# A float32 model kernel: where the attention values, the attention projection and the convolution's norm stand in the mixing layers

## What is computed

```python
u = h @ w_in[i]                                     # q, k, v, convolution input, two gates
y_attn = sliding_window_attention(q, k, v, sinks[i], rel_bias) @ w_attn_proj[i]
h1 = val * jax.nn.sigmoid(gate)                     # 512 channels
h1 = depthwise_conv(h1, dw) + db                    # 31 taps along the tokens
y_conv = jax.nn.silu(layer_norm(h1, g, b)) @ w_conv_proj[i]
mix = (jax.nn.sigmoid(ga) * y_attn + jax.nn.sigmoid(gc) * y_conv) @ w_out[i]
h = layer_norm(ALPHA * h + mix, ln1_g[i], ln1_b[i])
```

## Time and profile before

| | |
|---|---|
| median of 3 runs | 1739.08 us (1737.29 to 1739.76) |
| span of the profiled execution | 1735.9 us |
| its mean granted TensorE clock | 0.983 of full speed |
| TensorE busy | 1678.5 us, 97% of the span |
| VectorE busy | 1189.9 us, 69% |
| ScalarE busy | 949.9 us, 55% |
| GpSimd busy | 616.9 us, 36% |
| mean DMA rate | 196 GB/s; 326 to 346 GB/s from about 1345 us to about 1690 us |

### The profile page before, as it was taken

How to read it: one execution, slowest core, us unless ns; L and a number is a source line. 1 busy time by engine, 2 the same in 40 slices (tenths; PEclk the granted TensorE clock), 3 DMA queues, 4 the chain that set the end, 5 groups by cost and what they waited for, 6 DMA issues and landing times.

```text
span 1735.9 us, 29864 instructions
## 1 busy us (share of the span) xinstructions
PE 1678.5 (97%) x12148; PEld 1561.4 (90%) x12148; DVE 1189.9 (69%) x1766; ACT 949.9 (55%) x1298; POOL 616.9 (36%) x438
## 2 busy tenths in 40 slices
PE   8999999999989999999999999999899999999997
PEld 7988999998889999987999999988898888888885
DVE  5665655556555545897775555798777888788895
ACT  4556564335655634555454433545447777777774
POOL 4133442012324401133020001121047787886863
PEclk8999999999999999999999999999989999999999
DMA  8432445554334555532335544533327989888992
GB/s 297 190 120 98 160 173 183 190 177 166 120 122 170 195 184 183 177 128 98 130 122 198 180 173 170 171 139 121 111 109 281 338 332 338 326 332 330 346 344 111
DMA packets 50206, 339.90 MB, mean 196 GB/s; under 512 B 5575, under 2 KB 7839, under 8 KB 10351
## 3 DMA queue, kind: packets, MB, share of 16 engines
q1 hardware_dynamic: 47344, 328.79, 52.1%
q0 software_dynamic: 2720, 9.13, 1.7%
HBM read 336.76 MB, written 1.13 MB: 195 GB/s over the span
## 4 chain that ended last, share of the span: by engine, by line
PE 78%; DVE 10%; ACT 7%; issue 3%; POOL 2%; DMA 0%; DVEq 0%; SPq 0%; ACTq 0%; POOLq 0%
PE bank L481 13%; PE bank L483 13%; PE bank L482 13%; PE bank L906 4%; PE bank L907 4%; PE bank L908 4%; DVE CA L1896 3%; DVE wl L1570 3%; ACT wh L1125 3%; PE bank L617 3%; PE bank L618 2%; PE bank L619 2%; PE bank L937 2%; PE bank L939 2%; PE bank L938 2%
## 5 line engine op out<-in xcount | busy, mean ns | idle before, releaser
L1570 DVE TENSOR_TENSOR wl<-stg,wh 128x2048 fp32r<-128x2048 f32 (+1 forms) x310 | 680.9, 2202 | 260.9 <-ACT wh L1125 260.1
L1125 ACT ACTIVATE wh<-stg 128x2048 fp32r<-128x2048 f32 x310 | 592.1, 1911 | 210.0 <-PE bank L483 100.5
L481 PE MATMUL bank<-xh,wh 128*128 128x256 f32 (+1 forms) x1322 | 381.4, 288 | 3.2 <-DVE xl L1616 1.7
L483 PE MATMUL bank<-xh,wl 128*128 128x256 f32 (+1 forms) x1322 | 378.3, 286 | 0.0
L482 PE MATMUL bank<-xl,wh 128*128 128x256 f32 (+1 forms) x1322 | 377.3, 285 | 0.0
L2230 POOL TENSOR_TENSOR wl<-stg,wh 128x512 fp32r<-128x512 f32 x132 | 322.8, 2458 | 114.4 <-ACT wh L1125 96.1
L481 PEld LDWEIGHTS bank<-xh,wh 128*128 128x128 f32 x1322 | 250.7, 190 | 7.3 <-issue 6.6
L483 PEld LDWEIGHTS bank<-xh,wl 128*128 128x128 f32 x1322 | 250.8, 190 | 0.0
L482 PEld LDWEIGHTS bank<-xl,wh 128*128 128x128 f32 x1322 | 250.3, 189 | 0.1
L906 PE MATMUL bank<-wh,GH 128*128 128x512 f32 (+3 forms) x400 | 148.2, 370 | 1.5 <-ACT wh L1125 0.8
L908 PE MATMUL bank<-wl,GH 128*128 128x512 f32 (+3 forms) x400 | 146.5, 366 | 0.0
(11 more groups left out here) (319 smaller groups left out, 3438.4 us busy)
## 6 DMA issues: line engine op xcount, KB each, us to landing
stg<-in_w SPq DMA_DIRECT2D x310, 1024.0 KB, 4.8
BT<-bias_scratch POOLq DMA_DIRECT2D x3, 1024.0 KB, 11.0
BT<-bias_scratch POOLq DMA_DIRECT2D x1, 2048.0 KB, 13.0
BB<-bias_scratch POOLq DMA_DIRECT2D x2, 1024.0 KB, 7.4
res<-in_x SPq DMA_DIRECT2D x1, 1024.0 KB, 5.6
stg<-in_w SPq DMA_DIRECT2D x2, 512.0 KB, 7.1
BB<-bias_scratch POOLq DMA_DIRECT2D x2, 512.0 KB, 7.8
out<-res SPq DMA_DIRECT2D x4, 256.0 KB, 3.4
```

What stands on the lines that cost most here:

```text
L481: pe.matmul(out, wh, xh(kt), start=kt == 0, stop=False)
L483: ins = pe.matmul(out, wl, xh(kt), start=False, stop=kt == KT - 1)
L1125: act.activation(WH[u % NW][:, :], stg[u % NS][:, :], ACT.Copy).then_inc(*m.inc("w_high", u))
L1570: vec.tensor_tensor(WL[u % NW][:, 0:n], stg[u % NS][:, 0:n], WH[u % NW][:, 0:n].bitcast(F32), ALU.subtract).then_inc(*m.inc("w_low_v", u))
```

## The change

Three things are altered in the mixing layers.

1. The value products come two steps later than their turns (`BEHIND = DEEP + 2`), in the even steps and ahead of that step's scores and turns. So the pump of a tile first multiplies the values of jobs that were turned in the pump before. The first pump comes one output tile earlier (`FIRST_STEP = 13`).
2. `ap` starts right behind the gates. The four matmuls of the channel mean stand behind `ap`'s first tile and one matmul for the variance behind its fourth.
3. The convolution norm's variance is no longer summed token by token. ScalarE squares with the factor 1/512 in it, GpSimd adds the four tiles of squares (three additions), one matmul with ones sums them over all partitions and spreads the sum at once, and 1/deviation is worked out on whole 128 x 272 tiles: Ln and Exp on ScalarE, then one Newton step in three VectorE instructions. `token_sums`, `deviation`, the diagonals, their matmuls and the copy are gone for this norm, and a `memset` of two small columns too.

```diff
 AHEAD = 3
 DEEP = 5
+BEHIND = DEEP + 2
+FIRST_STEP = 13
...
                 def step(i):
+                    if i % 2 == 0 and 0 < i - BEHIND < len(jobs):
+                        values(i - BEHIND)
                     if i % 2 == 0 and i < len(jobs):
...
-                    v = i - DEEP - 1
-                    if v % 2 and v > 0:
-                        two = jobs[v - 1:v + 1]
...
                 name = f"c{l}"
-                for kt in range(4):
-                    if kt == 0:
+
+                def conv_sums(nt):
+                    if nt == 0:
                         b, old = bank((name, "mean"), ("mean", name))
                         vacant(old)
...
-                token_sums(name, 4, TILES2, "centred_sq", name)
+                        for kt in range(4):
+                            w.wait_ge(*m.of("conv_v", (l, kt, 30)))
+                            ins = pe.matmul(PS[b][:, 0:T], ones, a["CA"][:, kt, 0:T], start=kt == 0, stop=kt == 3)
+                        ins.then_inc(*m.inc("group", (name, "mean")))
+                    if nt == 3:
+                        b, old = bank((name, "var"), ("var_out", name))
+                        vacant(old)
+                        w.wait_ge(*m.of("conv_sq_added", (l, 3)))
+                        pe.matmul(PS[b][:, 0:T], ones, SQ[:, 0, :], start=True, stop=True).then_inc(*m.inc("group", (name, "var")))
+
                 gemm(4, KD, lambda kt: a["MH"][:, kt, lo:T], lambda kt: a["ML"][:, kt, lo:T], n, f"ap{l}", lambda nt: [("attn_gated", (l, nt))],
-                     halves_ready(f"a{l}"), lambda nt: along_columns(name) if nt == 1 else None)
+                     halves_ready(f"a{l}"), conv_sums)
...  ScalarE
-                mean(name, 4)
...
+                sp.enter(sp.at // UT)
+                w.wait_ge(*m.of("group", (name, "mean")))
+                act.activation(BC[:, :], bank((name, "mean"))[:, 0:T], ACT.Copy, scale=1.0 / (4 * P)).then_inc(*m.inc("mean", name))
+                for kt in range(4):
+                    w.wait_ge(*m.of("centred", (name, kt)))
+                    act.activation(SQ[:, kt, :], XC[:, kt, :], ACT.Square, scale=(4 * P) ** -0.5).then_inc(*m.inc("centred_sq", (name, kt)))
+                act.preload_act_table_set(LOG_EXP)
...
-                    if nt != 1:
+                    if nt != 3:
                         return
-                    spread(name, 4)
+                    w.wait_ge(*m.of("var_out", name))
+                    act.activation(SQ[:, 5, :], SQ[:, 4, :], ACT.Ln).then_inc(*m.step("table"))
+                    w.wait_ge(*m.last("table"))
+                    act.activation(BC[:, :], SQ[:, 5, :], ACT.Exp, scale=-0.5).then_inc(*m.inc("guess", name))
...  VectorE
+                def conv_var():
+                    w.wait_ge(*m.of("group", (name, "var")))
+                    vec.tensor_scalar(v, bank((name, "var"))[:, 0:T], LN_EPS, None, ALU.add).then_inc(*m.inc("var_out", name))
...
-                    if nt == 1:
-                        spread(name)
-                        scale_y(name, "clg", l, 4, low)
+                    if nt == 0:
+                        conv_centre()
+                    if nt == 2:
+                        conv_var()
+                    if nt == 3:
+                        conv_root()
+                        conv_scale()
...  GpSimd
+                for kt in range(1, 4):
+                    w.wait_ge(*m.of("centred_sq", (f"c{l}", kt)))
+                    if kt > 1:
+                        w.wait_ge(*m.of("conv_sq_added", (l, kt - 1)))
+                    pool.tensor_tensor(SQ[:, 0, :], SQ[:, 0, :], SQ[:, kt, :], ALU.add).then_inc(*m.inc("conv_sq_added", (l, kt)))
```

More of the change, by code:

```diff
@@ L739, in mix_layer, with values @@
                 tag, done, scored, opened = f"b{l}", [0], [], {}
+                def values(v):
+                    two = jobs[v - 1:v + 1]
+                    nq, c0, hp, n = two[0]["nq"], two[0]["c0"], two[0]["hp"], len(two[0]["chunks"])
+                    w.wait_ge(*m.of("turned_p", (tag, v, "all")))
+                    if v == 1:
+                        w.wait_ge(*m.of("v_turned", (l, 1)))
+                    if hp not in opened:
+                        opened[hp], old = bank(("pair", tag, hp), ("x_low", (f"a{l}", hp)))
+                        held.add(opened[hp])
+                        vacant(old)
+                    for c in range(n):
+                        for k in range(2):
+                            _, wide, val = two[k]["chunks"][c]
+                            ins = pe.matmul(PS[opened[hp]][64 * k:64 * k + 64, c0:c0 + nq], val,
+                                            a["PT"][(v - 1 + k) % 3][0:wide, c, 0:nq], start=c == 0, stop=c == n - 1)
+                    ins.then_inc(*m.inc("group", ("pair", tag, v)))
+                    if two[0]["tt"] == 1:
+                        let_go(opened[hp])
                 def step(i):
+                    if i % 2 == 0 and 0 < i - BEHIND < len(jobs):
+                        values(i - BEHIND)
                     if i % 2 == 0 and i < len(jobs):
@@ L1925, in mix_layer, with conv_centre, conv_root, conv_scale @@
                 walk_late(30, KD, evac)
-                centre(name, CA, 4)
-                for i in range(done[0], len(jobs) + DEEP + 1):
-                    front(i)
-                    back(i)
-                deviation(name, 4)
+                v, t = SQ[:, 4, :], SQ[:, 6, :]
+                def conv_centre():
+                    w.wait_ge(*m.of("mean", name))
+                    for kt in range(4):
+                        vec.tensor_tensor(XC[:, kt, :], CA[:, kt, 0:T], BC[:, :], ALU.subtract).then_inc(*m.inc("centred", (name, kt)))
+                def conv_var():
+                    w.wait_ge(*m.of("group", (name, "var")))
+                    vec.tensor_scalar(v, bank((name, "var"))[:, 0:T], LN_EPS, None, ALU.add).then_inc(*m.inc("var_out", name))
+                def conv_root():
+                    w.wait_ge(*m.of("guess", name))
+                    vec.tensor_tensor(t, BC[:, :], BC[:, :], ALU.mult).then_inc(*m.step("v_step"))
+                    w.wait_ge(*m.last("v_step"))
+                    vec.scalar_tensor_tensor(t, t, -0.5, v, ALU.mult, ALU.mult).then_inc(*m.step("v_step"))
+                    w.wait_ge(*m.last("v_step"))
+                    vec.scalar_tensor_tensor(BC[:, :], t, 1.5, BC[:, :], ALU.add, ALU.mult).then_inc(*m.inc("rstd", name))
+                    w.wait_ge(*m.last("rstd"))
+                def conv_scale():
+                    for kt in range(5):
+                        if kt < 4:
+                            vec.scalar_tensor_tensor(SQ[:, kt, :], XC[:, kt, :], small("clg", l * 4 + kt), BC[:, :], ALU.mult,
+                                                     ALU.mult).then_inc(*m.inc("normed_y", (name, kt)))
+                        if kt > 0:
+                            low(kt - 1)
                 def low(kt):
@@ L2198, in vector_program @@
             ffn_block(1)
-            vec.memset(st6[:, 0:2, 0:8], 1.0).then_inc(*m.step("v_step"))
-            w.wait_ge(*m.last("v_step"))
             split_norm("mean_e", "embg", "embb", 0)
```

88 lines of the change are left out of this document (13 added, 75 removed).

## The result

The changed kernel takes 1719.87 us (median of 4 runs, 1719.25 to 1722.57); the kernel before took 1738.18 us on the same chip (1736.23 to 1739.76). The ratio is 0.9897 with a 95% interval of 0.9884 to 0.991: 18.3 us faster, where 9.9 us were forecast.

What follows compares the result with a forecast made beforehand. TensorE was taken as the bound, except from the gates' end to `o`, where VectorE and ScalarE hand work to each other; 7.0 + 0.8 + 3.6 - 1.5 = 9.9 us off 1739.1 gave 1729.2 us, range 1724 to 1736.

Steps and rivals of the forecast that it cites:

- Part 1 gives 3.6 + 3.4 = 7.0 us: Gates of both mixing layers: value products read copies made a tile earlier, so 7.6 us of waits go; gain 7.0 us.
- VectorE's slack: Gates: VectorE can bear turns 0.8 to 1.0 us later; without slack in the second layer 3.4 us are lost.
- Part 2: From the end of the gates to `o`: an earlier first Silu gains 0.8 us in the first layer, 3.6 in the second.
- T0: The end of the gates, the zero from which the prediction timed `ap`, the norm and the first Silu.
- S: Time of the first Silu, expected 14.1 us (first layer) and 14.0 us (second) after the end of the gates.
- What is late next: Start of `o`: TensorE's wait of 1.9 us for the last low halves grows to 4 to 6 us in each layer.
- Half clock: Start of `o`: TensorE's clock may fall, 1.6 us a layer; 1.5 us taken, one layer of two, bounds 0 and 3.2.
- VectorE gives the first part back: Rival: the gates' gain is lost in the second layer and the clock falls in both; 1734.3 us, chance 0.14.
- only the waiting place moves: Rival: VectorE reaches the centring no earlier in either layer, 1.2 us left; 1737.9 us, no change, chance 0.12.
- turns wait for VectorE: Rival, slower: turns wait for banks `front` reads later, up to 0.9 us in each of 23 pumps; 1748 us, chance 0.07.
- the additions are not held up: Rival: GpSimd's additions slip in ahead of the split, first Silu 2 us earlier in each layer; 1725.2 us, chance 0.10.

Runs made afterwards that it cites:

- Part 1 alone: Kernel before with the changed kernel's later value products and earlier first pump, old norm and old place of `ap`: 1727.10 us, ratio 0.9934.
- part 2 alone: Changed kernel with the value products and first pump back in their old places: 1734.37 us, ratio 0.9992 to the kernel before.
- the filled wait: Kernel before with four spare matmuls ahead of the second value product of each mixing layer: 1736.60 us, ratio 0.9995.
- the second execution: The changed kernel once more, unaltered, on the same chip as the two runs beside it: 1720.93 us, ratio 0.9904 to the kernel before.
- the clock kept up at `o`: Changed kernel with spare matmuls before the waits of `o`'s first tile for its third to last operands: 1720.89 us, ratio 0.9907 to the kernel before.

## Why the prediction was wrong, step by step

**The step that failed is "Part 1 gives 3.6 + 3.4 = 7.0 us".** Its mechanism was right: the waits for `PTb` went, nothing was late in their place, and VectorE could bear it. Its size was taken from "7.6 us in 16 waits", the matmul records, while the weight loads waited 12.0 us (4.4 us of the miss). And the clock behind these waits was left out of the sum: two spells of 1.5 us (3.0 us). The prediction asked whether new waits would bring half clock and never whether the removed ones had, though its row of the gates gave the clock as 0.98, which over 69.88 us is about one such spell. Part 1 alone gave 14.4 us in the gates; part 2 alone showed the gates with the waits and without a spell, and the filled wait without either spell.

**VectorE's slack** held. Its waits for turns fell from 7.7 us to 4.2 in the first layer, those for `MH` from 5.0 and 4.6 to 1.6 and 1.3, as argued.

**Part 2** held to 0.3 us a layer: 13.83 and 14.10 us measured from the gates' end, 14.0 and 14.3 from T0, against 14.1 and 14.0. The additions took 4.46 and 4.77 us (forecast 4.6), though in the first layer the second of them was held up (2.62 us) and not the first (0.80). The page "GPSIMD Engine Reference" of the Trainium skill, section 8, has the contention with VectorE's instructions of two inputs; the trace agrees, and shows besides that VectorE pays too: that split took 2.87 instead of 2.28 us, though in the second layer it took 2.29. The table load of Silu, 823.86 to 825.14, is hidden beside the Newton step, and the Silu, 0.7 us behind it, is released by VectorE's scaling. The drain of the Trainium skill's page "ScalarE: Activation LUTs", section "What ACT_TABLE_LOAD costs", which would have made S 0.7 us later, is not seen in S: 14.04 us behind T0 against 14.1 without it.

**What is late next.** The waits for the mix came: 2.8 and 3.5 us by the matmul records, where 4 to 6 us a layer were named, but 4.5 and 5.0 us by the weight loads in 840 to 850 us and, behind the dots, in 1224 to 1234 us ("issue" is time for which the profile names no releaser):

```profile
PEld bank L483 <- ACT MH L1396: 3.4, 5, 0.8
PEld bank L483 <- issue: 1.1, 2, 0.7
...
PEld bank L483 <- ACT MH L1396: 3.6, 5, 1.1
PEld bank L483 <- issue: 1.4, 2, 0.7
```

Their size was right, and read from the same records that would have mended part 1. Half clock fell on both layers, 1.3 and 2.1 us (1.8 and 0.8 in the second execution), instead of one: 3.3 or 2.6 us where 1.5 were taken, about the upper bound of 3.2. It is the one term that was too small as a loss, and it hid 1 to 2 us of the first error.

**The rivals.** That VectorE gives the first part back and that only the waiting place moves are refuted by the gates and the Silu together; that turns wait for VectorE by the list of waits, which has no such row. That the additions are not held up is refuted too, but it had a point: GpSimd began 0.08 us ahead of the split and one addition slipped in, in the first layer only. Taking them off GpSimd gave about the 2 us a layer that this rival named. None of the rivals gave a time as low as the measured one, and none named the waits' true size.

**What stays open.** The two parts alone give 10.3 and 3.1 us by the medians, 13.4 together, and 12.4 and 2.7 us by the changed stretches, 15.1 together. In the changed kernel the changed stretches give 15.4 and 16.2 us in two executions, the medians 18.3 and 17.3. The half clock ahead of the first mixing layer and the wait for the input differ from one execution to the next, 700.1 to 705.3 us over all kernels here, and the kernel before ran between 1733.2 and 1745.4 us; the median of the changed kernel lies 2.0 us above its first profiled span and 0.5 us below the second, where that of the kernel before lay 3.2 above its own. Whether the change has a part in the last 1 to 3 us was not settled. Nor was it settled why the clock kept up at `o` doesn't show in the median. The profiled execution of that kernel is not a typical one: it is the fastest of its five runs (1718.22 us, mean clock 0.990), while the other four have 1720.71 to 1722.65 us and 0.986. By my estimate from that mean they spent some 14 us more at half clock, and no trace shows where.

## What to carry to other kernels

Read what a wait of TensorE costs from its weight loads, or from the distance of the first matmul behind a break to the last one ahead of it, and not from the matmul records, which showed 7.6 us where the weight loads showed 12.0 and the removal of the waits, the clock apart, gave 11.4. Look behind each wait that a change removes for half clock, as behind each that it adds. Where TensorE is covered for a stretch, the next gain is in the order of the other engines: a split moved on ScalarE alone gave 2.4 us a layer, and work that doesn't fit beside VectorE's splits is better on TensorE while TensorE has slack.

## What the hardware showed that I had not expected

In the gates of the first layer, a wait whose longest is 1.3 us by the weight loads was followed by 3.4 us of half clock in one execution and not in another that had the same waits (119.33 us with the spell, 117.85 without). Over all executions, 3 of 4 gate stretches with these waits had a spell and none of the 20 without them.

Ahead of the changed code, where all kernels here are the same, the executions differ by 5 us (700.1 to 705.3). Some 2 us of that are the wait of the first matmul for the input (6.8 to 8.9 us), the rest goes with 13.7 to 27.3 us of half clock.

Of GpSimd's three additions beside a VectorE split, one is held up until about 0.6 us past the split's end and the others keep their 0.75 to 0.80 us. In the second layer it is the first (2.98 us), and the split keeps its 2.29 us. In the first layer it is the second (2.62 us), and the split grows to 2.87 us. The additions started 0.07 and 0.08 us ahead of the split, and the second execution of the changed kernel repeats both layers to 0.01 us. Why the two layers differ was not tested.
